# Hybrid decoder layer: Scalar's copy of the turned stick-breaking weights moved ahead of the unit's first sigmoid

## What is computed

```
log_beta = log_sigmoid(z)
log_1m   = where(strict, log_sigmoid(-z), 0)
after    = reverse_cumsum(log_1m) - log_1m
w        = where(strict, exp(log_beta + after), 0)
out      = w @ v
```

## Time and profile before

| | before |
|---|---|
| median of 3 runs | 1345.55 us (1345.51 to 1346.98) |
| profiled execution | 1347.07 us, span 1345.3 us |
| TensorE busy | 1294.5 us, 96% of the span |
| VectorE busy | 807.8 us, 60% |
| Scalar busy | 560.6 us, 42% |
| scans, L1419 | 64, 86.5 us |
| first sigmoids, L924 | 64, 415.3 to 566.4 us into the span |
| granted clock of TensorE | 0.996 |

### The profile page before, as it was taken

How to read it: one execution, slowest core, us unless ns; L and a number is a source line. 1 busy time by engine, 2 the same in 40 slices (tenths; PEclk the granted TensorE clock), 3 DMA queues, 4 the chain that set the end, 5 groups by cost and what they waited for, 6 DMA issues and landing times.

```text
span 1345.3 us, 17161 instructions
## 1 busy us (share of the span) xinstructions
PE 1294.5 (96%) x6703; PEld 1076.1 (80%) x6703; DVE 807.8 (60%) x1098; ACT 560.6 (42%) x913; POOL 61.9 (5%) x69
## 2 busy tenths in 40 slices
PE   3999999999899999999999999999999999999998
PEld 2688887898788888888777888888888888887886
DVE  7534657687667988853679565656665543334333
ACT  4511312586446788851364333333333323222221
POOL 1100200121000001000000000000000000001001
PEclk9999999999999999999999999999999999999999
DMA  9253355200012234301232222122212155447443
GB/s 377 74 225 143 142 218 171 69 1 17 17 40 67 58 74 126 142 22 57 77 143 78 94 95 80 61 95 94 94 52 91 63 180 172 141 141 266 143 149 123
DMA packets 39389, 150.30 MB, mean 112 GB/s; under 512 B 4432, under 2 KB 4624, under 8 KB 37776
## 3 DMA queue, kind: packets, MB, share of 16 engines
q1 hardware_dynamic: 36976, 140.85, 30.7%
q0 software_dynamic: 2336, 8.39, 1.7%
HBM read 117.77 MB, written 24.12 MB: 105 GB/s over the span
## 4 chain that ended last, share of the span: by engine, by line
PE 86%; DVE 6%; ACT 3%; issue 2%; DMA 1%; POOL 1%; SPq 0%; DVEq 0%; ACTq 0%
PE ps L2204 28%; PE ps L1707 13%; PE ps L1696 10%; PE ps L1698 10%; PE ps L1697 10%; PE ps L1976 3%; PE ps L1963 2%; PE ps L1954 2%; PE ps L1921 1%; DVE left L1419 1%; PE ps L1922 1%; PE ps L1943 1%; PE ps L1740 1%; DVE beta L1424 1%; ACT omb L924 1%
## 5 line engine op out<-in xcount | busy, mean ns | idle before, releaser
L1696 PE MATMUL ps<-TH,dWH 128*128 128x512 f32 x352 | 137.1, 389 | 0.9 <-DVE yst L1671 0.9
L1698 PE MATMUL ps<-TH,dWL 128*128 128x512 f32 x352 | 137.0, 389 | 0.0
L1697 PE MATMUL ps<-TL,dWH 128*128 128x512 f32 x352 | 136.9, 389 | 0.0
L2204 PE MATMUL ps<-h2H,slH 128*128 128x512 f32 x320 | 124.6, 389 | 0.0
L2204 PE MATMUL ps<-h2L,slH 128*128 128x512 f32 x320 | 124.5, 389 | 0.0
L2204 PE MATMUL ps<-h2H,slL 128*128 128x512 f32 x320 | 124.5, 389 | 0.0
L1630 DVE TENSOR_TENSOR TL<-traw,TH 128x512 fp32r<-128x512 f32 x44 | 30.5, 693 | 134.4 <-ACT TH L1052 134.4
L1032 ACT ACTIVATE slH<-ssum 128x512 fp32r<-128x512 f32 x80 | 50.4, 632 | 140.4 <-PE ps L2204 96.4
L1052 ACT ACTIVATE TH<-traw 128x512 fp32r<-128x512 f32 x44 | 27.8, 632 | 164.0 <-PE ps L1698 157.3
L1419 DVE TENSOR_TENSOR_SCAN left<-omb 128x255 f32<-128x255 f32 (+4 forms) x64 | 86.5, 1352 | 9.5 <-ACT omb L924 8.6
L1696 PEld LDWEIGHTS ps<-TH,dWH 128*128 128x128 f32 x352 | 66.1, 188 | 15.3 <-DVE yst L1671 1.3
(11 more groups left out here) (328 smaller groups left out, 3013.0 us busy)
## 6 DMA issues: line engine op xcount, KB each, us to landing
ada<-ada SPq DMA_DIRECT2D x12, 2048.0 KB, 9.0
draw<-down SPq DMA_DIRECT2D x44, 512.0 KB, 3.6
sraw<-gu SPq DMA_DIRECT2D x20, 1024.0 KB, 6.0
raw<-win SPq DMA_DIRECT2D x22, 512.0 KB, 4.6
traw<-t_spill_d SPq DMA_DIRECT2D x44, 256.0 KB, 3.9
t_spill_d<-tst SPq DMA_DIRECT2D x20, 512.0 KB, 3.0
x_in<-xT SPq DMA_DIRECT2D x4, 1024.0 KB, 8.9
qkl_spill_d<-qkl SPq DMA_DIRECT2D x8, 512.0 KB, 3.5
```

Source lines behind the costliest of these rows:

```text
L1696: mm(out, lh, rh, start=first, stop=False)
L1697: mm(out, lh, rl, start=False, stop=False)
L1698: return mm(out, ll, rh, start=False, stop=last)
L2204: last = mm(ps[:, Q_BANK[q], :], l[q][:, w], r[:, c, :], start=(c == 0 and k == 0 and q not in (Q_G2, Q_S4)), stop=(c == 3 and k == 2), sk ...
```

## The change

From unit 3 on Scalar copies the turned weights of the unit two back at the start of a unit, ahead of its waits for the scores and ahead of the first sigmoid, and not between the two sigmoids. So the copies of units 1 to 61 move; that of unit 0, and those after the loop (units 62 and 63), stay where they were. No other engine's instructions change.

```diff
@@ stick_step(u), Scalar
             if u == 0:
                 act.wait_ge(sem["m_qk"], after(NM - 1))
+            if u >= 3:
+                stick_copy(u - 2)
             act.wait_ge(sem["s_qk"], after(u))
             act.wait_ge(sem["s_scan"], after(u - 2))
             A(omb[v % 2][:, 0:n], pair(2 * (v % 2), n), ACT.Sigmoid, scale=-(SBD ** -0.5)).then_inc(sem["s_nb"], 1)
             if u < 2:
                 mla_copy(NM - 2 + u, NU - 2 + u)
-            else:
-                if u == 2:
-                    act.wait_ge(sem["m_av"], after(NM - 1))
-                stick_copy(u - 2)
+            elif u == 2:
+                act.wait_ge(sem["m_av"], after(NM - 1))
+                stick_copy(0)
             act.wait_ge(sem["s_tr"], after(u - 2))
             A(beta[v % 2][:, 0:n], pair(2 * (v % 2), n), ACT.Sigmoid, scale=SBD ** -0.5).then_inc(sem["s_b"], 1)
```

## The result

The changed kernel takes 1379.22 us (median of 4 runs, 1375.96 to 1381.94) against 1345.53: a ratio of 1.0242 (95% interval 1.0221 to 1.0263), so 30 to 35 us slower. The profiled execution took 1378.53 us for a span of 1376.8, 31.5 more than the span before. The time lies outside the predicted range, 1360 to 1377, on the slow side.

The account below looks back on a forecast made before the run. The prediction took a latency loop between TensorE, Scalar and VectorE in the stick-breaking stage as the bound. Its terms 1.6 + 20.5 + 2.5 = 24.6 us on 1345.55 gave 1370.2, range 1360 to 1377.

Parts of the forecast that it names:

- Sixth, seventh and eighth step: Turns of 6, 7 and 8 blocks in each group: total delay 0.36, 1.80, 3.41 us; group 18.45 to about 21.9.
- Six loops: Six groups between the seven 8-block turns in the stick-breaking stage: 3.4 us more each, 20.5 in all.
- First unit: First 8-block unit, ahead of the six loops: late by turn(7) and copy(7) alone, 1.6 us.
- Last part: Last 34.33 us of the stick-breaking stage: 2.5 us more, an estimate with bounds 0 and 6.8.
- Gains: Earlier copies could free at most the 3.6 us that TensorE's turns wait for them; nothing was taken.
- Nothing given back after the stage: What follows the stage, from 572 us on, starts later by the same amount; TensorE there is nearly gapless.
- The Trainium skill's price of a copy: Scalar's copies of 7, 5, 4 blocks: 1.04, 0.83, 0.72 us by the skill; 0.7 more a loop, near 1375.
- The clock at 1.00: TensorE's granted clock in the changed profile was to stay at 1.00.
- the rival that did: Clock falls at TensorE's waits in seven groups, 3.0 us each, 21 in all, perhaps half hidden: 1380; chance 0.10.
- the prediction's own signs of being wrong: Wrong if a group is under 20 us, TensorE's lost time lies after the stage, or the clock fell.

Follow-up runs that it names:

- Experiments 3 to 5: Changed kernel with the early copy only before units of 8, of 7, and of 1 to 6 blocks: 1369.59, 1354.35 and 1350.89 us.
- experiment 2: Changed kernel plus 24 small matmuls on TensorE ahead of each 8-block turn except the last head's: 1373.7 us, ratio 1.0190 to the kernel before.
- experiment 3: Changed kernel with the early copy only before 8-block units, other copies between the sigmoids: 1369.59 us, ratio 1.0166 to the kernel before.
- experiment 9: Kernel before with Scalar's copy of the unit two back placed after both sigmoids: 1362.53 us, ratio 1.0117.
- experiments 1: Changed kernel plus 24 small matmuls on TensorE ahead of every 8-block turn: 1373.98 us, ratio 1.0218 to the kernel before.
- experiment 4: Changed kernel with the early copy only before 7-block units, other copies between the sigmoids: 1354.35 us, ratio 1.0060 to the kernel before.

## Why the prediction was wrong, step by step

- *Sixth, seventh and eighth step, 0.36, 1.44 and 1.61, a group of 21.86.* Right: 21.93 in the first group. Its turns came at 7.17, 15.37 and 21.93 after the 8-block turn; predicted 7.16, 15.32, 21.86. Experiments 3 to 5 give the three parts singly as 0.4, 1.2 and 1.6; the 0.3 missing to 3.5 is mostly the 0.27 that the 7-block delay loses when it comes alone.
- *Six loops, 20.5.* As far as the order goes, right to 1 us: 132.6 - 111.1 = 21.5 with the gaps filled (experiment 2), some of it the fill's own.
- *First unit 1.6.* Right (1.57).
- *Last part 2.5, an estimate, bounds 0 to 6.8.* Measured 4.0, of which 2.8 is order and 1.1 a fall of the clock (the stretches under experiment 2). The estimate was near.
- *Gains: nothing.* Right: the wait for wT went from 3.6 to 2.7 us and nothing came of it.
- *Nothing given back after the stage.* Right, 773.6 against 773.5.
- *The Trainium skill's price of a copy, 0.7 more a loop, near 1375.* Did not show: the first group took 21.93, not 22.6, and the copies 0.60, 0.70 and 0.92 us, as in the old trace. The row that the prediction cites ("ScalarE: Activation LUTs", section "Rules for kernel authors" of the Trainium skill) is for an activation whose bias is a [128,1] pointer operand; these copies have no such bias, so it was the wrong price for them. That it gives a time near the measured one is chance.
- *The clock at 1.00.* **This step failed.** The sum held no term for it, and the rival that did had a chance of 0.10; a fall of the clock was also one of the prediction's own signs of being wrong. The gap was predicted well (2 us; it was 2.05), and I set it against a gap of 1.66 us that did nothing and one of 1.93 that was followed by a fall, and took the side of the harmless one because matmuls stood close around it. That was no ground: the gap was longer than both. In the profiled execution the clock fell behind five of the seven 8-block turns. Four of them are in groups, and against the same groups with filled gaps they cost 23.28 - 22.00, 23.15 - 21.99, 23.42 - 22.51 and 23.55 - 22.06: 0.9 to 1.5 us each, 4.8 in all. The fall in the last part cost 1.1 more. The rival's 1380 was nearer the result than the forecast, in part by luck: it had seven falls (there were five) of 3.0 us with half hidden, so 1.5. The falls were half as long as the one at the start of the old trace (some 3.5 us and 7), so at half the clock each could cost half of 3.5, about 1.75, and most of that was paid, not half.

Together: order 1.6 + 21.5 + 2.8 = 25.9, clock 4.8 + 1.1 = 5.9, earlier start -0.4: 31.4 of the 31.5 measured. Without the clock's 5.9 the profiled execution would have taken some 1372.6 us (1378.53 - 5.9), inside the range.

The four executions fit this: spans of 1374.2, 1376.8, 1378.1 and 1380.1 go with granted clocks of 0.993, 0.991, 0.989 and 0.988. So how much the clock costs differs between executions of one kernel. Only one of the four was traced; why its first and fourth 8-block turn were spared is open.

## What to carry to other kernels

A wait put at the head of an in-order engine's queue is paid by all that stands behind it; look whether what it waits for is issued, on its own engine, after the very thing that the next instruction needs. Here that doubled up, since copy, sigmoid, scan, product and turn became one line twice a group. And a gap on TensorE has two prices: the gap, and what the clock does behind it. When a change makes TensorE wait longer than any gap that the old trace shows without a fall, some falls belong into the sum, with a wide range. Shorter waits are not safe either: two of 1.34 us and two of 1.40 had falls behind them here, though one of 1.66 never had.

## What the runs showed of the hardware

A wait of 2.05 us, in groups in which TensorE is busy 18.2 of 21.9 us, was followed by a clock of 0.5 in five of seven cases, and in experiment 3 in four of seven. Behind a wait of 1.40 us (experiment 9) it was two of seven; behind one of 1.34 us in the last part one each in experiments 1 and 2, and none in the changed kernel and experiment 3; behind waits of 1.12 us (experiment 4) none. A wait of 1.66 us in the MLA stage had no fall behind it in any of the twelve traces, and the one at the start, followed by a fall in the old trace (1.93), had none in experiments 1 and 4 (1.88). So the length of a wait does not settle it. That the clock falls behind waits agrees with the rule that the idle state is the throttled one ("TensorE: Matmul & The Clock Gate", Part 1 of the Trainium skill); which waits, these runs do not explain.

A fall of some 3.5 us cost 0.9 to 1.5 us, one of some 7 us 2.7 to 3.0. Small matmuls without use, put into the gap of 2.05 us, left waits of at most 0.7 and held the clock at all seven turns, in both experiments that had them.
